# GpSimd's halvings of weight units in four instructions of 512 columns

## The reference

```
proj = h @ w_in
ret  = _retention(rq, rk, rv, positions) * silu(rg)
y    = _ssd(xs, dt, A, Bm, Cm) + d_skip[:, None] * xs
fox  = _forgetting_attention(fq, fk, fv, log_f) * silu(fg)
return x + gate * (concatenate([ret, ssd, fox]) @ w_out)
```

```
x = layer_norm(ALPHA * x + 0.5 * swiglu(x, ffn_wg[l, 0], ffn_wu[l, 0], ffn_wd[l, 0]), ...)
m = token_mix(x, w_in[l], w_out[l], ...)
x = layer_norm(ALPHA * x + m, ...)
x = layer_norm(ALPHA * x + 0.5 * swiglu(x, ffn_wg[l, 1], ffn_wu[l, 1], ffn_wd[l, 1]), ...)
```

## Time and profile before

| | us |
|---|---|
| median of 3 runs | 3245.23 (3244.2 to 3250.93) |
| the profiled execution's own time | 3239.83 |
| its span | 3238.0 |
| TensorE busy | 3083.6 (95%) |
| VectorE busy | 1341.3 (41%) |
| GpSimd busy | 1248.8 (39%) |
| ScalarE busy | 947.4 (29%) |

### The profile page before, as it was taken

One profiled execution on the slowest core, in us unless ns is written; L12 is line 12 of the kernel. 1 busy time (PEld: TensorE's weight loads), 2 busy tenths in 40 slices (PEclk: granted clock), 3 DMA queues, 4 the chain that ended last, 5 costly groups with the idle time before them and its releaser, 6 DMA issues. The chain is left out here.

```text
span 3238.0 us, 40354 instructions
## 1 busy us (share of the span) xinstructions
PE 3083.6 (95%) x16100; PEld 2523.3 (78%) x16100; DVE 1341.3 (41%) x2025; ACT 947.4 (29%) x1679; POOL 1248.8 (39%) x400
## 2 busy tenths in 40 slices
PE   4999989999998999999989999999999998999998
PEld 4878977788887788887757888888888775788886
DVE  6557544836735122233366322232222337632223
ACT  3356443336544111102455211011110245421101
POOL 1423325323233454444341444444444434154442
PEclk9999999999999999999999999999999999999999
DMA  5323214322230222232210222232223221022222
GB/s 230 118 78 111 83 54 173 133 72 104 80 106 28 89 94 96 86 97 96 78 41 14 91 91 98 82 106 91 91 88 99 85 79 40 27 79 97 93 89 71
DMA packets 45865, 287.86 MB, mean 89 GB/s; under 512 B 5496, under 2 KB 6008, under 8 KB 18680
## 3 DMA queue, kind: packets, MB, share of 16 engines
q1 hardware_dynamic: 42624, 270.58, 23.7%
q10 hardware_dynamic: 3096, 15.27, 1.4%
HBM read 283.67 MB, written 2.16 MB: 88 GB/s over the span
## 5 line engine op out<-in xcount | busy, mean ns | idle before, releaser
L1882 PE MATMUL PS<-x_parts,w_parts 128*128 128x512 f32 x4224 | 961.0, 390 | 4.1 <-ACT x_parts L727 4.1
L1823 POOL TENSOR_TENSOR w_parts<-w_raw,w_parts 128x2048 fp32r<-128x2048 f32 (+1 forms) x152 | 644.5, 4240 | 811.1 <-DVE w_parts L1957 756.6
L1882 PEld LDWEIGHTS PS<-x_parts,w_parts 128*128 128x128 f32 x4224 | 793.3, 188 | 173.4 <-issue 4.9
L136 POOL TENSOR_TENSOR w_parts<-w_raw,w_parts 128x2048 fp32r<-128x2048 f32 (+1 forms) x98 | 449.4, 4587 | 964.2 <-ACT w_parts L127 930.1
L329 PE MATMUL PS<-x_parts,w_parts 128*128 128x512 f32 x2784 | 693.5, 395 | 13.6 <-POOL w_parts L136 4.6
L329 PEld LDWEIGHTS PS<-x_parts,w_parts 128*128 128x128 f32 x2784 | 519.5, 189 | 133.3 <-issue 18.7
L1923 PE MATMUL PS<-hidden_parts,w_parts 128*128 128x512 f32 x2112 | 482.9, 390 | 0.0
L1923 PEld LDWEIGHTS PS<-hidden_parts,w_parts 128*128 128x128 f32 x2112 | 396.1, 188 | 83.9 <-issue 1.9
L1964 DVE TENSOR_TENSOR ffn_buffers<-PS,ffn_buffers 128x512 f32<-128x512 f32 x88 | 60.9, 692 | 732.0 <-PE PS L1882 708.9
L332 PE MATMUL PS<-w_parts,x_parts 128*128 128x256 f32 x2304 | 294.3, 288 | 2.2 <-POOL w_parts L136 2.2
L332 PEld LDWEIGHTS PS<-w_parts,x_parts 128*128 128x128 f32 x2304 | 282.5, 193 | 15.2 <-issue 11.6
(11 more groups left out here) (393 smaller groups left out, 3157.5 us busy)
## 6 DMA issues: line engine op xcount, KB each, us to landing
w_raw<-in_w_gu SPq DMA_DIRECT2D x88, 1024.0 KB, 4.7
w_raw<-in_w_in SPq DMA_DIRECT2D x70, 1024.0 KB, 4.8
w_raw<-in_w_d SPq DMA_DIRECT2D x64, 704.0 KB, 4.0
w_raw<-in_w_out SPq DMA_DIRECT2D x24, 1024.0 KB, 4.7
m_all<-in_w_next SPq DMA_DIRECT2D x14, 1024.0 KB, 8.4
m_all<-in_w_gate SPq DMA_DIRECT2D x8, 1024.0 KB, 4.7
ssd_buffers<-decay_rows ACTq DMA_DIRECT2D x16, 512.0 KB, 4.4
m_all<-in_w_next ACTq DMA_DIRECT2D x2, 1024.0 KB, 11.7
```

What stands on the lines that cost most here:

```text
L136: pool.tensor_tensor(parts[:, self.slot(u), 1, 0:n], raw[:, self.slot(u), 0:n], parts[:, self.slot(u), 0, 0:n].bitcast(F32), ALU.subtract) ...
L1823: pool.tensor_tensor(WP[:, b, 1, 0:n], RAW[:, b, 0:n], WP[:, b, 0, 0:n].bitcast(F32), ALU.subtract).then_inc(self.low, 1)
L1882: return pe.matmul(PS[:, 2 * b + g, :], WP[:, slot(b), w, c:c + P], XS[:, x, k, :], start=start, stop=stop)
```

## The change

Both places that halve a unit now do it in a loop of instructions of at most 512 columns: four for a unit of 2048, three for 1408 (512, 512 and 384), two for 1024. The wait stands before the first and the semaphore's step behind the last. Nothing else differs; lines behind the first place move by four, behind the second by seven.

```diff
+LOWERED = 512
...
             pool.wait_ge(self.high, u + 1)
-            pool.tensor_tensor(parts[:, self.slot(u), 1, 0:n], raw[:, self.slot(u), 0:n],
-                               parts[:, self.slot(u), 0, 0:n].bitcast(F32), ALU.subtract).then_inc(self.low, 1)
+            for at in range(0, n, LOWERED):
+                to = min(n, at + LOWERED)
+                last = pool.tensor_tensor(parts[:, self.slot(u), 1, at:to], raw[:, self.slot(u), at:to],
+                                          parts[:, self.slot(u), 0, at:to].bitcast(F32), ALU.subtract)
+            last.then_inc(self.low, 1)
...
                 pool.wait_ge(self.high, count)
-                pool.tensor_tensor(WP[:, b, 1, 0:n], RAW[:, b, 0:n], WP[:, b, 0, 0:n].bitcast(F32),
-                                   ALU.subtract).then_inc(self.low, 1)
+                for at in range(0, n, LOWERED):
+                    to = min(n, at + LOWERED)
+                    last = pool.tensor_tensor(WP[:, b, 1, at:to], RAW[:, b, at:to], WP[:, b, 0, at:to].bitcast(F32),
+                                              ALU.subtract)
+                last.then_inc(self.low, 1)
```

## The result

The changed kernel takes 3218.35 us, the median of four runs (3218.13 to 3222.66); the kernel before, on the same chip, 3247.55 (3244.2 to 3250.93). The ratio is 0.9917, 95% interval 0.9904 to 0.993: 27 us faster. It is inside the predicted range of 3217 to 3243, but only 1.35 us above its low end, 13 us under the predicted 3231.

The account below looks back on a forecast made before the run. TensorE bounds the kernel, waiting at places for VectorE operations held up by GpSimd's halvings. The terms sum to -14 us, from a median of 3245.23 to 3231 us, with a range of 3217 to 3243.

Parts of the forecast that it names:

- R1: Rival: VectorE does not get in between GpSimd's pieces and waits 5.05 us instead of 4.5; +11 us, 3256 us; chance 0.08.
- Input norm: Before the first matmul, once: L582 and L583 get in between pieces, TensorE starts 5.5 us earlier, part given back; -3.5 us.
- The give-back of 2: At the input norm: the second halving's four pieces lengthen the norm's own two-input operations by some 0.5 each, 2.0 us.
- Retention: Each layer: four waits for L921 go (-3.4), TensorE waits for later halvings (+3.8 and +0.6); +1 us in sum.
- Chunk scan: Each layer: of L1170's waits for L1480, four behind caught VectorE operations shrink or go; -7 us, middle of 4.5 and 9.2.
- Scan's end: At L1538, four operations beside a halving: four pieces for four operations give the same end; 0 us.
- waits for a halving: TensorE's six waits for a late halving: the four that nothing takes up grow by 0.5 us each; +2 us.
- Second mixer: Each layer: L2514 is no longer caught, -2.4 us, and L2271's waits behind L2580 go, -4.1 us.
- Feed-forward: Four times: each halving's 0.5 us growth is hidden by some 4 us before TensorE needs the unit; 0 us.
- R2: Rival: slips make halvings late, and retention's eight units cost TensorE 15 us in place of 4.4; 3242 us; chance 0.18.
- A sign of being wrong: The prediction would be wrong if TensorE's waits for L139, the halving's new line, summed to over 15 us.
- R3: Rival: TensorE comes earlier to its next wait for ScalarE, so the -7 and -2.4 are lost; 3240.6 us; chance 0.12.

Follow-up runs that it names:

- ret_only: Against the kernel before, only the first six units of each retention are halved in pieces of 512 columns; ratio 1.0009 to the kernel before.
- mixer2_only: Against the kernel before, only eight units in each of the two later mixers are halved in pieces of 512 columns; ratio 0.9986.
- ffn_only: Against the kernel before, only the feed-forward parts' units (152 of 250) are halved in pieces of 512, the mixers' units whole; ratio 0.9989.
- all_but_scan: Against the changed kernel, the four units per layer under VectorE's scan chain and the feed-forward units are whole again; ratio 0.9973 to the kernel before.

## Why the prediction was right, and by how much it was off

The mechanism was right: VectorE gets in between pieces.'s single L1544 had shown it, and L2587, L586 and L587 repeat it, all under 1.5 us. R1 is refuted: VectorE comes in before GpSimd's next piece. The Trainium skill (page "GPSIMD Engine Reference", section "Instruction dispatch") says that a core starts the next instruction as soon as its own share of the last is done. Taken strictly, as I took it for R1, that would leave no gap for VectorE; the page doesn't speak of VectorE there, these rows show a gap, and the measurement decides.

- *Input norm*, predicted -3.5: TensorE starts 6.07 us earlier (59.45 to 53.38), near the 5.5 of the working. The give-back of 2 was the wrong step: measured by itself the norm is -6.8, with an interval (3.6 to 10.1) that makes a full give-back unlikely, not impossible.
- *Retention*, +1: +1.1 in the waits of ret_only. The third unit's wait and the end of those for L921 came as worked out (1.8 us at the first).
- *Chunk scan*, -7: the waits fall by 8.5 us, the rest by 9.0 with only the scan in pieces. Right for the waits, but the kernel gains 18 there.
- *Scan's end*, 0, and *waits for a halving*, +2: not measured alone. L1202's 3.2 us of waits are gone, and waits for L139 took their place: of the 12.4 us by which the waits for a halving grew, 2.7 are the norm's (L304), 4.5 retention's and 0.8 L336's (0.4 each where 0.5 was predicted), so 4.4 are left for the scan's end and the other units at L333.
- *Second mixer*, -2.4 and -4.1: both waits for L2580 go (4.1), and of L2218's 2.9 only 1.6, not 2.4. But L2205's 1.4 us of waits for L2524, on which the prediction said nothing, go too: -7.1, or -6.3 with L336's growth, where mixer2_only's rest fell by 6.7.
- *Feed-forward*, 0: ffn_only's interval holds 1, and among TensorE's waits there is none of L1889 or L1930 for L1829.
- R2, halvings made late by slips: the waits for a halving are 19.2 us, over the 15 at which I had said that the prediction would be wrong. They cost less than they look, since 3.4 at L921 and 3.2 at L1202 went in exchange. A sign of being wrong was thus set too tight for a prediction that held; so was VectorE's busy time (84 us less, not 100), and a piece took 1.36 (feed-forward) and 1.43 us (mixers) in the mean, not 1.26. R3, gain not passed on: in the scan none of it was lost.

The sum was -14. TensorE's waits fell by 16.8: some 2 more at the norm and 1.5 more in the scan than predicted, and the other differences nearly cancel. What was missing is a term, TensorE's clock, which the sum puts at nothing: the loss fell by 12.2, and less the 3.4 of the norm's start, which the waits count already, that is some 9 us of the medians' 29. Waits and clock make 26 of the 29; the last 3 can't be told from the noise of four runs. In the two profiled executions the clock hardly shows, because that of before happened to lose only 42.7, some 10 less than the mean of its runs, where that of the changed kernel lost 38.9; the two traces differ by 21.3 us, the medians by 29. I had noticed that the profiled execution of before was 5.4 us under the median and carried the difference over as a constant. It was not a constant but, in large part, low clock that the change takes away.

That the time still lies in the range is luck. The low end, 3217, came from costs left out and from 5 us for waits behind ScalarE that I had not priced; none of it stands for the clock, and without it the time would have been outside. The mechanism was right, the size was half of what was measured.

A small view of what the clock costs is behind L2580. The window of the kernel before, just behind TensorE's wait of 2.1 us there, and below it that of the changed kernel at nearly the same work:

```profile
1658.00:1661.00 3.00, 3.00 (x5) 1.03 (x4) 0.81 (x4) 0.58 (x1) 0.00 (x0) 0.50 0.70 295
```

```profile
1642.00:1645.00 3.00, 3.00 (x7) 0.78 (x5) 0.12 (x2) 1.75 (x3) 0.67 (x1) 1.00 0.35 101
```

At 0.50 (1.2 GHz) TensorE gets through five matmuls, at 1.00 (2.4 GHz) seven. The eight matmuls of L2278 (L2285 in the changed kernel) take 5.54 us and 3.85. A little later the changed kernel has its low clock too (0.50 for 6.8 us from 1647.2), but TensorE stands idle for ScalarE in the first 2.4 us of it. From the eight matmuls to L2343 (L2350) it takes 22.3 us before and 20.8 after: in this place the wait cost its 2.1 us and 1.5 more, though the low-clock loss of both is the same 3.4.

## What to carry to other kernels

Where one engine's long instruction holds another up, find in the trace one case in which the other got in between two short ones: that row was enough to predict the mechanism. Then price three things apart: what TensorE stops waiting for, what the cut instruction costs where it is itself waited for (here 5.1, 5.7 and 6.7 us for two, four and eight pieces in the mixers, 4.7 whole), and the clock. Cut only as fine as the first needs: 1024 did as well as 512, and 256 gave nearly everything back. And take the mean granted clock of all the runs shown, not only of the profiled one, before carrying a trace's sum over to a median.

## What was not expected of the hardware

A wait of TensorE in a dense stretch can cost more than its length. With waits of 11.1 and 17.5 us put back, and nothing else of GpSimd's or TensorE's work changed, the runs lost 9.5 and 15.8 us more to the low clock: nearly as much again. This fits what the Trainium skill says (page "TensorE: Matmul & The Clock Gate", section "Part 1: The HAM clock gate"), that the array's clock depends on how busy it has been. It isn't a fixed price for a wait: with pieces of 1024, 4 us more of the scan's waits stayed (8.7 in six, in place of 4.7 in four) and the loss was the same 40.2 (in the traces 1.7 us at the scan), and in the second mixer 7.1 us of waits went and the mean loss did not fall. Which waits bring it is left open; so is what share the dummy work itself has, though all_but_scan, without any, lost 9.5 more too.

Cutting costs more than the fixed price I had worked out from instructions of 512 columns (5.05 us for four). In the feed-forward part, where VectorE is less dense, a unit of 2048 columns took 4.95 us whole, 5.06 in two pieces (2.531 each), 5.43 in four (1.357) and 6.2 in eight (0.778). In the mixers it was 4.68, 5.1, 5.7 and 6.7. And VectorE's instructions beside a train of pieces are slowed one by one: an operation of 1024 columns takes 1.22 us with GpSimd idle, and the ten dummy operations, all beside pieces, took 1.48 to 2.20, with a median of 2.17.
